# Two more units with chunks by seven products, the MLP loops written out, and VectorE's operations on pairs of PSUM banks joined

## The reference

```
h = rmsnorm(x) ; proj = h @ w_in                      # sparse attention A, window attention B
merged = sigmoid(h Wg_A) * (o_A W_A) + sigmoid(h Wg_B) * (o_B W_B)
x = x + merged @ w_out
h = rmsnorm(x)
x = x + square(relu(h @ w_up)) @ w_down                # w_up: 2048 x 8192, w_down: 8192 x 2048
```

## Time and profile before

| | |
|---|---|
| time, median of 3 runs | 2674.16 us (2673.42 to 2676.18) |
| the profiled execution, its own time | 2673.84 us |
| its span, first to last instruction | 2672.1 us |
| TensorE's granted clock, mean | 0.999 of full speed |
| TensorE busy | 2657.7 us |
| VectorE, ScalarE, GpSimd busy | 2058.7, 1445.5, 127.6 us |
| HBM read and written | 573 MB, 215 GB/s |

### The profile page before, as it was taken

How to read it: one execution, slowest core, us unless ns; L and a number is a source line. 1 busy time by engine, 2 the same in 40 slices (tenths; PEclk the granted TensorE clock), 3 DMA queues, 4 the chain that set the end, 5 groups by cost and what they waited for, 6 DMA issues and landing times.

```text
span 2672.1 us, 37287 instructions
## 1 busy us (share of the span) xinstructions
PE 2657.7 (99%) x13576; PEld 2232.1 (84%) x13576; DVE 2058.7 (77%) x3051; ACT 1445.5 (54%) x1863; POOL 127.6 (5%) x218
## 2 busy tenths in 40 slices
PE   9999999999999999999999999999999999999998
PEld 7788778888888888888888887788888888888887
DVE  5676568977898897987756755689678988989875
ACT  5545555545565555645445455555456556556554
POOL 0100000000100100100010000000001001000000
PEclk9999999999999999999999999999999999999999
DMA  7885545676775766766687655466677767667574
GB/s 259 235 238 169 178 162 187 225 238 236 236 232 194 238 219 208 240 205 236 227 234 227 219 175 172 161 200 225 228 252 234 229 205 239 209 218 233 190 248 152
DMA packets 179961, 575.56 MB, mean 215 GB/s; under 512 B 23016, under 2 KB 43028, under 8 KB 179664
## 3 DMA queue, kind: packets, MB, share of 16 engines
q1 hardware_dynamic: 166256, 536.94, 61.3%
q0 software_dynamic: 13008, 35.98, 5.1%
q10 hardware_dynamic: 528, 0.37, 0.1%
HBM read 535.15 MB, written 38.04 MB: 215 GB/s over the span
## 4 chain that ended last, share of the span: by engine, by line
PE 92%; DVE 4%; DMA 2%; ACT 1%; issue 1%; SPq 0%; POOLq 0%; POOL 0%; ACTq 0%
PE acc L527 24%; PE acc L529 23%; PE acc L528 23%; PE att L495 2%; PE att L497 2%; PE att L496 2%; PE acc L495 2%; PE acc L497 2%; PE acc L496 2%; PE acc L544 1%; PE acc L543 1%; PE acc L545 1%; DVE w_lo L1311 1%; DMA raw<-in_w_main 1%; DVE w_lo L1332 1%; PE turn L496 1%
## 5 line engine op out<-in xcount | busy, mean ns | idle before, releaser
L1311 DVE TENSOR_TENSOR w_lo<-raw,w_hi 128x1024 fp32r<-128x1024 f32 (+1 forms) x778 | 934.8, 1212 | 410.9 <-ACT w_hi L886 409.0
L886 ACT ACTIVATE w_hi<-raw 128x1024 fp32r<-128x1024 f32 (+1 forms) x778 | 813.4, 1051 | 655.8 <-PE acc L529 485.9
L527 PE MATMUL acc<-w_hi,h_hl 128*128 128x512 f32 x1848 | 736.2, 398 | 0.4 <-DVE w_lo L1311 0.3
L529 PE MATMUL acc<-w_hi,h_hl 128*128 128x512 f32 x1848 | 729.0, 394 | 0.0
L528 PE MATMUL acc<-w_lo,h_hl 128*128 128x512 f32 x1848 | 728.5, 394 | 0.0
L527 PEld LDWEIGHTS acc<-w_hi,h_hl 128*128 128x128 f32 x1848 | 347.9, 188 | 82.7 <-issue 4.6
L529 PEld LDWEIGHTS acc<-w_hi,h_hl 128*128 128x128 f32 x1848 | 347.9, 188 | 81.3
L528 PEld LDWEIGHTS acc<-w_lo,h_hl 128*128 128x128 f32 x1848 | 348.3, 188 | 76.0
L1332 DVE TENSOR_TENSOR w_lo<-raw,w_hi 128x1792 fp32r<-128x1792 f32 x166 | 335.5, 2021 | 38.7 <-ACT w_hi L895 37.8
L527 PE MATMUL acc<-w_hi,o_hl 128*128 128x512 f32 x912 | 360.9, 396 | 0.0
L528 PE MATMUL acc<-w_lo,o_hl 128*128 128x512 f32 x912 | 359.9, 395 | 0.0
(11 more groups left out here) (298 smaller groups left out, 3504.7 us busy)
## 6 DMA issues: line engine op xcount, KB each, us to landing
raw<-in_w_main SPq DMA_DIRECT2D x928, 512.0 KB, 4.2
scratch<-spread SPq DMA_DIRECT2D x37, 512.0 KB, 2.7
moved<-scratch SPq DMA_DIRECT2D x148, 128.0 KB, 3.2
scratch<-spread POOLq DMA_DIRECT2D x30, 512.0 KB, 3.6
moved<-scratch POOLq DMA_DIRECT2D x120, 128.0 KB, 4.9
raw<-in_w_misc SPq DMA_DIRECT2D x16, 336.0 KB, 4.4
bias_b<-bias_rows POOLq DMA_DIRECT2D x32, 96.0 KB, 5.7
xs<-in_x SPq DMA_DIRECT2D x4, 512.0 KB, 7.2
```

Source lines behind the costliest of these rows:

```text
L527: nc.tensor.matmul(o, a_hi, hi[:, kk], start=(k == 0), stop=False)
L529: last = nc.tensor.matmul(o, a_lo, hi[:, kk], start=False, stop=fin)
L886: nc.scalar.activation(w_hi[s][:, 0:2 * width], raw[r][:, 0:2 * width], ACT.Copy).then_inc(hi_ready, 1)
L1311: nc.vector.tensor_tensor(w_lo[s][:, 0:2 * width], raw[r][:, 0:2 * width], w_hi[s][:, 0:2 * width].bitcast(F32), ALU.subtract).then_inc(lo ...
```

## The change

1. `WIDE_UP[1]` becomes (1, 3): the second up unit of the next group, at the end of each turn, has two chunks by seven products. `WIDE_FIRST = (5, 7)` does the same for the second up unit ahead of the groups. Their sides go to the banks `att[2]` and `turn`, those of the third up unit now to `att[0]` and `att[1]` (`SIDES_OF_UP`).
2. The second up block so needs `add_up_sides`: VectorE adds behind chunk 3 of the third up unit. ScalarE copies a side before chunk 3, and takes relu and square before chunk 6 (before chunk 4 in the last group); before it took the block whole, before chunk 5 (chunk 3 in the last group). The transpose moves from behind chunk 4 to behind chunk 6 (in the last group from behind chunk 3 to behind chunk 4).
3. `u_moved(g, 0)` of both engines moves from behind chunk 2 of the third up unit to behind chunk 7 of the second up unit that comes ahead of it. The sums of that block are split earlier, too.
4. The loops of SP, ScalarE and VectorE over the three turns are written out.
5. PSUM is allocated in pairs of banks. Where VectorE worked on two banks or two row tiles in two operations of 512 columns, it does one of 1024: the transpose, both gate products, the addition to x, the addition of down sides, and the last addition of `add_up_sides`.

The core of the diff (the counters that follow from it, and lines that only repeat these forms, are left out):

```diff
-WIDE_UP = ((1, 3, 5), (), (1, 3, 5, 7), ())
+WIDE_UP = ((1, 3, 5), (1, 3), (1, 3, 5, 7), ())
+WIDE_FIRST = (5, 7)
+SIDES_OF_UP = (0, 1, 0)
...
-            return ctx.enter_context(nc.psum_tensor(name, [P, NB], F32))
+            return ctx.enter_context(nc.psum_tensor(name, [P, TT * NB], F32))[:].rearrange("p (t c) -> p t c", t=TT)
...
-                with sp.Fori(0, GROUPS - 1) as g:
+                for g in range(GROUPS - 1):
...
-                up(C_MLP + 8, 1, adds(0, 0), 1)
+                up(C_MLP + 8, 1, adds(0, 0), 1, [(c, h_sums_took, (G_SUMS + H_SUMS) * l + G_SUMS + c // 2 + 1) for c in WIDE_FIRST],
+                   WIDE_FIRST)
...
-                    up(g * 64 + (C_MLP + 72), 1, adds(g, 3), 1)
+                    up(g * 64 + (C_MLP + 72), 1, adds(g, 3), 1, wide=WIDE_UP[1])
...
-                run(C_MLP + 8, {3: lambda: take_up(0, 0, base + 8, 0)}, {1: lambda: h_sums(3)})
-                with act.Fori(0, GROUPS - 1) as g:
+                run(C_MLP + 8, {3: lambda: take_up(0, 0, base + 8, 0)}, {1: lambda: h_sums(3), 7: lambda: u_moved(0, 0)},
+                    WIDE_FIRST, steps_at(0, -len(WIDE_FIRST)))
+                for g in range(GROUPS - 1):
                     end = g * 64 + base
-                    run(g * 64 + (C_MLP + 16), {5: lambda: take_up(g, 1, end + 16, 1)},
-                        {2: lambda: u_moved(g, 0), 7: lambda: u_sums_hi(g, 0)}, WIDE_UP[2], steps_at(g, AT_UP2))
+                    run(g * 64 + (C_MLP + 16), {3: lambda: take_side(g, 1, end + 16), 6: lambda: take_summed(g, 1, sides_count(g, 0))},
+                        {0: lambda: u_sums_hi(g, 0)}, WIDE_UP[2], steps_at(g, AT_UP2))
...
-                    run(g * 64 + (C_MLP + 72))
+                    run(g * 64 + (C_MLP + 72), (), {7: lambda: u_moved(g, 4)}, WIDE_UP[1], steps_at(g, AT_UP1))
                 g, end = GROUPS - 1, base + 64 * (GROUPS - 1)
-                run(C_MLP + 64 * g + 16, {3: lambda: take_up(g, 1, end + 16, 1)}, {2: lambda: u_moved(g, 0)},
-                    WIDE_UP[2], steps_at(g, AT_UP2))
+                run(C_MLP + 64 * g + 16, {3: lambda: take_side(g, 1, end + 16), 4: lambda: take_summed(g, 1, sides_count(g, 0))},
+                    (), WIDE_UP[2], steps_at(g, AT_UP2))
...
-                for t in range(TT):
-                    last = nc.vector.transpose(spread[:, :, :, t, :].rearrange("p j k s -> p k j s"),
-                                               src[:, t, :].rearrange("p (k j s) -> p k j s", k=PIECES, j=QUARTERS))
-                last.then_inc(spread_ready, 1)
+                nc.vector.transpose(spread[:].rearrange("p j k t s -> p t k j s"),
+                                    src.rearrange("p t (k j s) -> p t k j s", k=PIECES, j=QUARTERS)).then_inc(spread_ready, 1)
...
-                    nc.vector.tensor_tensor(stage[:, 0, :], acc[0][0][:], stage[:, 0, :], ALU.add)
                     dve.wait_ge(up_step, steps + 3)
-                    nc.vector.tensor_tensor(stage[:, 1, :], acc[0][1][:], stage[:, 1, :], ALU.add).then_inc(up_summed, 1)
+                    nc.vector.tensor_tensor(stage[:], bank, stage[:], ALU.add).then_inc(up_summed, 1)
...
-                run(C_MLP + 8, {2: factors}, {1: lambda: h_sums(3), 3: lambda: spread_u(0, 0)})
-                with dve.Fori(0, GROUPS - 1) as g:
+                run(C_MLP + 8, {2: factors}, {1: lambda: h_sums(3), 3: lambda: spread_u(0, 0), 7: lambda: u_moved(0, 0)},
+                    WIDE_FIRST, steps_at(0, -len(WIDE_FIRST)))
+                for g in range(GROUPS - 1):
                     end = g * 64 + base
                     run(g * 64 + (C_MLP + 16), (),
-                        {2: lambda: u_moved(g, 0), 4: lambda: spread_u(g, 1), 7: lambda: u_sums_lo(g, 0)}, WIDE_UP[2], steps_at(g, AT_UP2))
+                        {1: lambda: u_sums_lo(g, 0), 3: lambda: add_up_sides(g, 1, NBLK), 6: lambda: spread_u(g, 1)},
+                        WIDE_UP[2], steps_at(g, AT_UP2))
...
-                    run(g * 64 + (C_MLP + 72), (), {5: lambda: take_down(g, 3, end + 72)})
+                    run(g * 64 + (C_MLP + 72), (), {5: lambda: take_down(g, 3, end + 72), 7: lambda: u_moved(g, 4, g < GROUPS - 2)},
+                        WIDE_UP[1], steps_at(g, AT_UP1))
                 g = GROUPS - 1
-                run(C_MLP + 64 * g + 16, (), {2: lambda: u_moved(g, 0, False), 3: lambda: spread_u(g, 1)},
+                run(C_MLP + 64 * g + 16, (), {3: lambda: add_up_sides(g, 1, NBLK), 4: lambda: spread_u(g, 1)},
                     WIDE_UP[2], steps_at(g, AT_UP2))
```

More of the change, by code:

```diff
@@ L84 @@
 WIDE_AT = tuple(AT_DOWN + sum(len(w) for w in WIDE[:n]) for n in range(NBLK))
-N_WIDE = AT_DOWN + sum(len(w) for w in WIDE)
+AT_UP1 = AT_DOWN + sum(len(w) for w in WIDE)
+N_WIDE = AT_UP1 + len(WIDE_UP[1])
 WIDE_GATE = (1, 3, 5, 7)
@@ L187, in trunk_kernel @@
         last_gain = bias_a[:].rearrange("p h s -> p (h s)")
[L189 to L192, removed]
+        acc_pair = [psum(f"acc{s}") for s in range(2)]
+        acc = [[pair[:, t, :] for t in range(TT)] for pair in acc_pair]
+        wide_pair = [psum("att01"), psum("att2_turn")]
+        wide_acc = [[pair[:, t, :] for t in range(TT)] for pair in wide_pair]
+        att, turn = [*wide_acc[0], wide_acc[1][0]], wide_acc[1][1]
         idx_banks = wide_acc
@@ L827, in up @@
                     unit(l * CHUNKS + at, 8, h_lhs, acc[bank], None, before, hold=hold, wide=wide, sum_of=h_sum,
-                         sides=wide_acc[n // 2])
+                         sides=wide_acc[SIDES_OF_UP[n]] if wide else None)
                 def down(at, bank, before, n, hold=(), wide=()):
@@ L1730, in add_to_x @@
                     bank = n % 2 if bank is None else bank
-                    for t in range(TT):
-                        xb = xs[:, t, cols(n)]
-                        if scale is None:
-                            last = nc.vector.tensor_tensor(xb, acc[bank][t][:], xb, ALU.add)
-                        else:
-                            last = nc.vector.scalar_tensor_tensor(out=xb, in0=acc[bank][t][:], scalar=scale, in1=xb,
-                                                                  op0=ALU.mult, op1=ALU.add)
-                    last.then_inc(dve_took, 1)
+                    xb = xs[:, :, cols(n)]
+                    if scale is None:
+                        summed = nc.vector.tensor_tensor(xb, acc_pair[bank], xb, ALU.add)
+                    else:
+                        summed = nc.vector.scalar_tensor_tensor(out=xb, in0=acc_pair[bank], scalar=scale, in1=xb,
+                                                                op0=ALU.mult, op1=ALU.add)
+                    summed.then_inc(dve_took, 1)
                 def spread_x(e, n, units):
@@ L1813, in take_sides @@
                 def take_sides(n):
[L1815 to L1816 removed]
+                    nc.vector.tensor_tensor(rest[:, n], wide_pair[1 - n % 2], rest[:, n], ALU.add)
                 def add_sides(n):
```

47 lines of the change are left out of this document (22 added, 25 removed).

## The result

| | before | after |
|---|---|---|
| median of 6 runs each, alternating | 2674.38 us (2672.67 to 2676.18) | 2691.76 us (2688.78 to 2697.41) |
| ratio, 95% interval | | 1.0066 [1.0055, 1.0076] |
| the profiled execution, its own time and span | 2673.84, 2672.1 us | 2693.02, 2690.9 us |

The change makes the kernel 17.4 us slower (forecast 12.5). The page of after has these lines where the page of before has the earlier trace rows: the engines' busy times, then groups of instructions (busy us, mean ns, idle before).

The account below looks back on a forecast made before the run. TensorE's pace was taken as the bound, with VectorE's and ScalarE's work hidden while their lead lasts. Terms 8.9 + 3.6 + 0.4 + 4.4 - 4.8 = 12.5 us longer gave 2686.5 us, range 2679.5 to 2695.

Parts of the forecast that it names:

- First new stall: Start of the first group's third up unit: TensorE waits for the moved block's landing, 3.3 and 5.6 us, together 8.9.
- rival (d): Steady groups: VectorE becomes the bound there too, 1 to 2 us in each of 4 groups, 2690 to 2695 us; chance 0.14.
- The gain: TensorE: 16 chunks go from 2.78 to 2.48 us each by seven products, 4.8 us less.
- VectorE pays: Per new chunk, three sums and a wider split: 2.33 us more, 37 us in all, costing time only without lead.
- The joins and loops: Joined 1024-column operations and written-out loops: both costed at 0, since TensorE did not wait at those places.
- Rival (b): Loop edges: branch idle was worth time, 4 x 2.52 = 10.1 us less, 2676.4 us, or 2659 with (a); chance 0.03.
- Second new stall: Chunks 0 to 4 of the first group's third up unit: VectorE needs 12.6 us against TensorE's 10.5; 3.6 us in all.
- Steady groups: Second and third group of each layer: lead covers the work, 0.6 us in hand at the third up unit's chunk 4; 0.
- Last groups: Last group's third and fourth up units: earlier take of the summed block and later transfer, 2.2 us a layer, 4.4.
- Rival (c): All stalls half as long as forecast: 3.9 us more, 2677.9 us, no measurable change; chance 0.08.
- (a): Whole kernel: all the gain and no stall, 2669.2 us; chance 0.05.
- (e): New chunks don't run at 2.48 us or hold TensorE for sums of h: gain shrinks to nothing, 2691.3 us; chance 0.02.

Follow-up runs that it names:

- e6: Kernel before with joins and written-out loops, plus seven-product chunks only in second up blocks of groups two and three, in e3's order; 2672.67 us, ratio 0.9993.
- e1: Kernel before with PSUM in pairs, joined operations and loops written out, without the new chunks; 2675.91 us, ratio 0.9994.
- e3: Changed kernel with the second up block's relu and square before chunk 5 and its transpose behind chunk 4, in all groups; 2689.98 us, ratio 1.0044 to before.
- e8: e3 with the last group's second block taken over behind chunk 3 of the fourth up unit, not chunk 2; 2685.31 us, ratio 1.0041 to before.
- e9: e6 with the first group's first-block take-over moved from behind chunk 2 of the third up unit to chunk 7 of the second; 2686.25 us, 1.0039 to before.
- e5: Changed kernel keeping only the first group's new chunks (WIDE_FIRST) and order, with later second up units plain; 2687.84 us, ratio 1.0049 to before.
- e4: Changed kernel with the moves of both e2 and e3; 2686.33 us, ratio 1.0033 to before.
- e2: Changed kernel with the first block's take-over put back behind chunk 2 of the third up unit, first group only; 2695.5 us, ratio 1.0071 to before.
- e7: e4 with, in the first group, sides added up behind chunk 4 and the transpose behind chunk 6; 2685.98 us, ratio 1.0041 to before.
- e11: e9 with the first block taken over one chunk later, behind chunk 0 of the third up unit; 2675.24 us, ratio 1.0002 to before.

## Why the prediction was right, and where it was wrong

Right: the sign, the range (2679.5 to 2695.0, measured 2691.8), the first stall with its path, and what does nothing. But one of the prediction's own signs of being wrong came true: stalls stand in the steady groups. The measured time is 5.3 us above the forecast and in the band of rival (d); it is inside the range because the upper end allowed 4 us for steady groups.

- **The gain**, 16 x 0.30: -4.7 measured.
- **VectorE pays** 2.33 us a chunk, hidden unless the lead is gone: e6 shows it hidden but for 0.3 us a group.
- **The joins and loops**, costed at 0: e1, ratio 0.9994. Rival (b), 10 us from the branch idle, is refuted, since the idle went and the time stayed. It also counted too many edges: VectorE stood idle with nothing to wait for at two of the four taken edges only (2.52 and 2.80 us, both in layer 0). The Trainium skill (Runtime: NRT & Kernel Launch, section "Instruction fetch mechanics") has the stall only for a taken branch whose target is outside the pages already fetched. The trace agrees in so far as some edges stall and others don't, and no idle is left in e1; which targets were outside, no run shows. It has no price here, as the edge was never on TensorE's path. The last addition behind the sides saves nothing, as argued: the four operations now run 1107.49 to 1110.26 in VectorE's timeline of the third group, 2.77 us against 2.72.
- **First new stall**, 8.9 forecast, 10.5 measured. The path of 5.95 us from the landing to the first matmul was 691.44 - 685.38 = 6.06 and 2026.58 - 2020.53 = 6.05. The landing in layer 0 was taken as 685.0 on the clock of before and measured 684.7 (TensorE would have begun at 691.44 - 3.09 = 688.35, where before's begins at 688.24 - 0.60, so 0.71 us are to be taken off); the wait 3.1 for 3.3. In layer 1 I took 2013.0 and it was 2020.53 - 9.42 = 2011.1, at the early bound: the wait 3.8 for 5.6. The term that was missing is TensorE's clock, 1.8 us behind each wait. That the layer 1 sum came out right (5.6 for 5.6) is chance.
- **Second new stall**, 3.6 forecast, 1.2 measured. VectorE's side was right: from the start of chunk 0's split to that of chunk 4's it took 702.79 - 690.07 = 12.7 us, and 2037.93 - 2025.22 = 12.7 in layer 1, for 12.6. TensorE's side was mis-sized: with the slow clock its four chunks took 1.8 us more than the 10.5 of the prediction, so that 0.3 to 0.6 us were left to wait. At full clock TensorE would have waited about 12.7 - 10.5 = 2.2 us at chunk 4 (an estimate from these rows), so the slow clock cost after almost nothing on top; it made the first step larger and the second smaller. The two stalls together are 11.7 us for 12.5.
- **Steady groups**, 0 forecast, 3.3 measured, in three of the four, and 2.2 more at the same place of the two first groups: this step failed. The tightest place was looked for at chunk 4 of the third up unit, and there the 0.6 us in hand held: no steady group waits there. But I did not follow the block on. Its transpose moved two chunks later, the place where ScalarE takes over its transfer didn't move, and the wait on that semaphore (4.97 us) used up the lead, to be paid where the next sides are added if a second wait comes in between. Nor did I price it in the first group. Rival (d) had the size (2690 to 2695) with another mechanism, VectorE's load; e3 and e6 show that the load fits, but for the 0.3 us, and the late transfer doesn't.
- **Last groups**, 4.4 forecast, 5.5 measured; the term counts the take-over in the fourth up unit as 0.5 us a layer, and it was 1.5 in layer 0 (0.75 + 0.74) and 0.4 in layer 1; in e8, with the take-over one chunk later, it is nothing in both. The third up unit, 1.7 forecast, took 1.8 in each layer, and 0.3 in e3, with relu and square one chunk later.
- **Rival (c)**, stalls half as long, did not come; (a) and (e) are out by the ledger.

## What to carry to other kernels

Where engines run their queues in written order, a step that waits for a transfer should be placed by its landing, and when its producer is moved later the consumer has to move too: e9's cost comes from one such step with nothing else changed, e3 removes most of the steady loss by moving the producer back, and e8 the last group's by moving the consumer on. Ask of each new wait not only how long it is but whether the lead that it uses is rebuilt before the next wait and the next tight place. And introduce a new method block by block: eight of these 16 chunks cost next to nothing, and the first group's four cost more than twice what all sixteen save.

## What the runs showed of the hardware that I had not expected

**TensorE's clock after a wait.** Behind each of the eight waits of 3.0 to 5.1 us in after, e3, e5, e8 and e9 the granted clock fell to the lower level for some 3 to 7 us, at a price of 1.6 to 2.7 us where it was read off. Of shorter waits some were followed by a fall (2.55 and 2.66 in e4, 1.92 and 2.64 in e2, 1.82 in e8), others of 1.5 to 2.6 us in e5, e7, e8 and e11 by none. What decides among these was not tried. A wait of 3 us so cost about 5 in e9, where nothing else held TensorE; in after the next wait was shorter by nearly as much. That idle gaps of TensorE bring the slow clock back, the Trainium skill says too (TensorE: Matmul & The Clock Gate, section "Why this matters for your kernels"); I had priced the waits without it.

**The scatter of one transfer.** Against the end of the second up unit the first block landed 3.0 and 2.2 us ahead in after (layers 0 and 1), 2.4 and 0.9 ahead in e9, and 1.0 behind in layer 1 of before, with the transpose behind the same chunk in all of them. These are different kernels with one trace each, so part of the 4 us may come from the weight loads, which run out where ScalarE stands still (in e9, 12 GB/s from 2016 to 2018 us, just before the landing). The scatter may be why the runs of after spread over 8.6 us and those of before over 3.5; that was not tested.
